# The second norm's root moved behind the first twelve up tiles of a hybrid decoder layer

## The reference

```python
    x = x + gate1 * (merged @ w_out)
    h2 = rms_norm(x, g_norm2) * (1.0 + scale2) + shift2
    x = x + gate2 * (jnp.square(jax.nn.relu(h2 @ w_up)) @ w_down)
```

## Time and profile before

| | us |
|---|---|
| runs shown (3) | 993.21, 993.28, 996.12; median 993.28 |
| profiled execution, its own time | 994.64 |
| profiled execution, span from first to last instruction | 992.9 |
| TensorE busy | 944.4 |
| VectorE busy | 497.6 |
| ScalarE busy | 391.0 |
| mean granted TensorE clock | 0.981 |

### The profile page before, as it was taken

One profiled execution on the slowest core, in us unless ns is written; L12 is line 12 of the kernel. 1 busy time (PEld: TensorE's weight loads), 2 busy tenths in 40 slices (PEclk: granted clock), 3 DMA queues, 4 the chain that ended last, 5 costly groups with the idle time before them and its releaser, 6 DMA issues.

```text
span 992.9 us, 19815 instructions
## 1 busy us (share of the span) xinstructions
PE 944.4 (95%) x7546; PEld 862.0 (87%) x7546; DVE 497.6 (50%) x1154; ACT 391.0 (39%) x813; POOL 139.5 (14%) x139
## 2 busy tenths in 40 slices
PE   8889989889899989899999999999999999999998
PEld 7588667767688768798799998999999999999997
DVE  3454767845625678861147556544332244443232
ACT  3254545555556646433333323433311233441121
POOL 4100232141334564310000000000000000000000
PEclk9889999999999989999999999999999999999999
DMA  9536764253422564587423331333223323322312
GB/s 322 186 107 194 185 226 129 96 160 124 132 65 73 167 207 131 158 256 252 143 65 95 98 86 43 85 87 103 86 86 102 87 85 90 100 85 88 103 43 86
DMA packets 176233, 124.54 MB, mean 125 GB/s; under 512 B 14739, under 2 KB 152019, under 8 KB 176164
## 3 DMA queue, kind: packets, MB, share of 16 engines
q1 hardware_dynamic: 176034, 123.50, 40.9%
q10 hardware_dynamic: 130, 0.10, 0.0%
HBM read 116.99 MB, written 6.59 MB: 124 GB/s over the span
## 4 chain that ended last, share of the span: by engine, by line
PE 66%; issue 20%; DVE 9%; ACT 3%; POOL 1%; POOLq 0%; ACTq 0%; DVEq 0%
PE bank L949 18%; PE bank L950 17%; PE bank L951 17%; PE bank L1030 2%; PE bank L1053 2%; PE bank L856 2%; PE bank L1039 2%; PE bank L1009 1%; PE bank L1071 1%; DVE sel L1878 1%; PE bank L878 1%; PE bank L1015 1%; PE bank L1094 1%; PE bank L1084 1%; DVE lg L1905 1%
## 5 line engine op out<-in xcount | busy, mean ns | idle before, releaser
L949 PE MATMUL bank<-h_hi,w_hi 128*128 128x260 f32 x1360 | 397.5, 292 | 8.0 <-DVE h_lo L1762 6.0
L950 PE MATMUL bank<-h_lo,w_hi 128*128 128x260 f32 x1360 | 388.5, 286 | 0.0
L951 PE MATMUL bank<-h_hi,w_lo 128*128 128x260 f32 x1360 | 388.1, 285 | 0.0
L949 PEld LDWEIGHTS bank<-h_hi,w_hi 128*128 128x128 f32 x1360 | 260.1, 191 | 31.6 <-issue 24.0
L951 PEld LDWEIGHTS bank<-h_hi,w_lo 128*128 128x128 f32 x1360 | 260.5, 192 | 0.0
L950 PEld LDWEIGHTS bank<-h_lo,w_hi 128*128 128x128 f32 x1360 | 260.2, 191 | 0.0
L949 PE MATMUL bank<-u_hi,w_hi 128*128 128x260 f32 x512 | 145.2, 284 | 0.0
L950 PE MATMUL bank<-u_lo,w_hi 128*128 128x260 f32 x512 | 144.8, 283 | 0.0
L951 PE MATMUL bank<-u_hi,w_lo 128*128 128x260 f32 x512 | 144.8, 283 | 0.0
L2213 DVE TENSOR_TENSOR w_lo<-raw,w_hi 128x1024 fp32r<-128x1024 f32 x62 | 76.0, 1226 | 135.2 <-ACT w_hi L1638 135.2
L1638 ACT ACTIVATE w_hi<-raw 128x1024 fp32r<-128x1024 f32 x62 | 65.4, 1055 | 140.3 <-PE bank L951 140.3
(11 more groups left out here) (316 smaller groups left out, 1180.9 us busy)
## 6 DMA issues: line engine op xcount, KB each, us to landing
raw<-in_w_in SPq DMA_DIRECT2D x44, 512.0 KB, 4.0
part<-in_w_ada SPq DMA_DIRECT2D x32, 512.0 KB, 5.4
raw<-in_w_up SPq DMA_DIRECT2D x32, 512.0 KB, 4.1
raw<-in_w_down SPq DMA_DIRECT2D x32, 512.0 KB, 4.1
ada<-in_w_ada SPq DMA_DIRECT2D x4, 2048.0 KB, 13.7
kv<-in_cache_k_b SPq DMA_DIRECT2D x16, 256.0 KB, 4.3
qbc<-q_d SPq DMA_DIRECT2D x16, 256.0 KB, 4.5
kv<-in_cache_k_a SPq DMA_DIRECT2D x16, 256.0 KB, 4.2
```

Source lines behind the costliest of these rows:

```text
L949: mm(out, hi[:, k, :], x_h, start=first and k == ks[0], stop=False)
L950: mm(out, hi[:, k, :], x_l, start=False, stop=False)
L951: end = mm(out, lo[:, k, :], x_h, start=False, stop=last and k == ks[-1])
```

## The change

The norm is rewritten around the product. With r the root of a token, W the up weights and s the scale times `g_norm2`, h2 W = r · ((x·s) W) + shift W. So twelve up tiles (`N_UNNORMED`) multiply x·s, without the root, and the root comes in afterwards, on the sums.

- **Inputs.** `scale_half` multiplies each chunk of `x_t` by `amul` inside the round of the `w_out` tile that made it. ScalarE rounds it to `h2_hi` there; the remainder `h2_lo` of the first half is taken in the same round, that of the second half in the next tile's (`rest_half`). Ten more columns (`N_C`) in front hold the shift, so the first half of such a tile has 270 columns, the second 260.
- **Order on TensorE.** Up tile 0 runs alone and chunk by chunk, with `norm_sums` between its chunks 4 and 5. `spread_roots` stands between the halves of up tile 1. `warm` is gone behind the sums.
- **Results.** VectorE takes the sums out of the bank with a multiply by `rs_row`, adds a correction for the 8 sample tokens, and ScalarE applies the ReLU with the shift as its bias.
- **The other up tiles.** `h3_hi` and `h3_lo`, which hold the normed inputs, are made chunk by chunk by both engines beside up tiles 2 to 10. Tiles 12 to 15 and the second quarter read them.
- **Weights.** `rest_w(T_MLP + 1)` stands ahead of `norm_root`, `rest_w(T_MLP + 2)` behind it. In the rounds of the `w_out` tiles ScalarE's `round_w` comes between the two halves.
- **Memory.** `u_hi` moves to the place of `h_hi` and `h_lo`.

```diff
@@ pe
-            norm_sums()
-            warm(10, 7)
-            spread_roots()
-            warm(8, 7)
+            def up_half(i, half, ks):
+                n0, n = (0, N_C + HALF) if half == 0 else (N_C + HALF, HALF)
+                out = bank[half + 4 * ((i + 1) % 2)][:, 0:n]
...
-            first_tiles(T_MLP, 1)
-            up_tile(0, 2, 0)
-            up_tile(0, 3, 0)
+            for i in (T_MLP, T_MLP + 1):
+                pe.wait_ge(hi_ready, i + 1)
+                pe.wait_ge(lo_ready, i + 1)
+                pe.wait_ge(dve_evac, 2 * (2 * NCH + i - T_MLP - 1))
+                if i == T_MLP:
+                    for k in range(NCH):
+                        pe.wait_ge(h2_lo_ready, 2 * k + 3)
+                        for half in range(2):
+                            up_half(i, half, [k])
+                        if k == 4:
+                            norm_sums()
+                else:
+                    up_half(i, 0, range(NCH))
+                    spread_roots()
+                    up_half(i, 1, range(NCH))
+            for n in range(2, N_UNNORMED):
+                pe.wait_ge(hi_ready, T_MLP + n + 1)
+                pe.wait_ge(lo_ready, T_MLP + n + 1)
+                for half in range(2):
+                    pe.wait_ge(u_evac, 2 * (n - 2) + half + 1)
+                    up_half(T_MLP + n, half, range(NCH))
+            pe.wait_ge(h3_lo_ready, NCH + 1)
             for q in range(2):
-                with pe.Fori(0 if q else 1, 4) as it:
+                with pe.Fori(0 if q else N_UNNORMED // 4, 4) as it:
@@ act
+                for half in range(2):
+                    if half and m < NCH - 1:
+                        round_w(i + 2)
+                    act.wait_ge(hf_ready, 2 * m + half + 1)
+                    A(h2_hi[:, m, ...], hf[:, m % 2, ...], ACT.Copy)\
+                        .then_inc(h2_hi_ready, 1)
+                square(m)
             round_w(T_MLP + 1)
-            round_h()
+            round_w(T_MLP + 2)
+            act.wait_ge(rs_spread2, 1)
+            A(rs_row[:, SEQ:T], bank[6][:, 0:NS], ACT.Copy)
+            A(rs_row[:, 0:SEQ], bank[3][:, :], ACT.Copy).then_inc(rs_kept, 1)
...
+            for n in range(N_UNNORMED):
+                if n:
+                    round_w(T_MLP + n + 2)
+                for half in range(2):
+                    if half == 0:
+                        act.wait_ge(u_evac, 2 * n + 1)
+                    else:
+                        act.wait_ge(z_ready, n + 1)
+                    uf = u_f[:, 2 * (n % 2) + half, :]
+                    A(uf, uf, ACT.Relu, bias=ws[:, n % 2, 0:1]).then_inc(act_evac, 1)
+                up_round(0, n % 4, n // 4)
...
@@ dve
                 for half in range(2):
                     dve.wait_ge(proj_done, 2 * (T_WO + g) + half + 1)
                     add_gated(bank[half + 4 * (g % 2)], half, slice(m, m + 1), slice(16 + m, 17 + m), m)
+                    scale_half(m, half)
+                    if half:
+                        rest_half(m, 0)
+                    elif m:
+                        rest_half(m - 1, 1)
...
+            rest_half(NCH - 1, 1)
+            rest_w(T_MLP + 1)
             norm_root()
-            norm_apply()
+            rest_w(T_MLP + 2)
+            dve.wait_ge(rs_kept, 1)
...
+            for n in range(N_UNNORMED):
+                first_up_tile(n)
+                if n:
+                    rest_w(T_MLP + n + 2)
+                up_squares(0, n % 4, n // 4)
+                j = n - 2
+                if j == 0:
+                    norm_samples()
+                if 0 <= j < NCH:
+                    norm_chunk(j)
+                up_rest(0, n % 4, n // 4)
+                if 0 <= j - 1 < NCH:
+                    rest_chunk(j - 1)
```

More of the change, by code:

```diff
@@ L1638, in round_loop, with up_round @@
                 A(w_hi[:, i % SPL], raw[:, i % RAW], ACT.Copy).then_inc(hi_ready, 1)
+            def up_round(q, b, it):
+                n = 32 * q + 2 * b
+                for half in range(2):
+                    act.wait_ge(u_sq, it * 8 + (n + half + 1))
+                    A(u_hi[:, bass.ds(it * 4 + b, 1), half * HALF:(half + 1) * HALF], u_f[:, 2 * (b % 2) + half:2 * (b % 2) + half + 1, :],
+                      ACT.Copy).then_inc(u_hi_ready, 1)
             def up_tile(q, b, it):
@@ L1653, in _ @@
             for q in range(2):
-                if q == 0:
+                with act.Fori(0 if q else N_UNNORMED // 4, 4) as it:
                     for b in range(4):
[L1656 to L1664, removed]
+                        up_tile(q, b, it)
@@ L1795, in scale_rows @@
                                        vec_t[:, 56:64].unsqueeze(2).to_broadcast([P, NCH, 9]), ALU.mult))
[L1797 to L1816, removed]
-                        dve.tensor_tensor(h_lo[:, :, SEQ:T], nsm[:, 0], h_hi[:, :, SEQ:T].bitcast(F32), ALU.subtract).then_inc(h_lo_ready, 1)
-                    else:
-                        dve.wait_ge(nf_ready, N_H + j + 1)
-                        rest_shifted(j - 1)
-                rest_shifted(NCH - 1)
@@ L2213, in rest_loop, with first_up_tile @@
                 dve.tensor_tensor(w_lo[:, i % SPL], raw[:, i % RAW], w_hi[:, i % SPL].bitcast(F32), ALU.subtract).then_inc(lo_ready, 1)
+            def first_up_tile(n):
+                i = T_MLP + n
+                at = 4 * ((i + 1) % 2)
+                for half in range(2):
+                    dve.wait_ge(proj_done, 2 * i + half + 1)
+                    if half == 0:
+                        dve.tensor_copy(ws[:, n % 2, :], bank[at][:, 0:N_C])
+                        acc = bank[at][:, N_C:N_C + HALF]
+                    else:
+                        acc = bank[at + 1][:, 0:HALF]
+                    dve.tensor_tensor(u_f[:, 2 * (n % 2) + half, :], acc, rs_row[:, half * HALF:(half + 1) * HALF], ALU.mult)\
+                        .then_inc(u_evac, 1)
+                dve.wait_ge(u_evac, 2 * n + 2)
+                us = u_f[:, 2 * (n % 2) + 1, HALF - NS:HALF]
+                dve.tensor_tensor(us, us, ws[:, n % 2, 1:9], ALU.add).then_inc(z_ready, 1)
@@ new lines, in up_squares, with up_rest @@
+            def up_squares(q, b, it):
+                for half in range(2):
+                    uf = u_f[:, 2 * (b % 2) + half, :]
+                    dve.wait_ge(act_evac, it * 8 + (2 * T_WO + 32 * q + 2 * b + half + 1))
+                    dve.tensor_tensor(uf, uf, uf, ALU.mult).then_inc(u_sq, 1)
+            def up_rest(q, b, it):
+                for half in range(2):
+                    slot = 2 * (b % 2) + half
+                    cols = slice(half * HALF, (half + 1) * HALF)
+                    dve.wait_ge(u_hi_ready, it * 8 + (32 * q + 2 * b + half + 1))
+                    dve.tensor_tensor(u_lo[:, bass.ds(it * 4 + b, 1), cols], u_f[:, slot:slot + 1, :],
+                                      u_hi[:, bass.ds(it * 4 + b, 1), cols].bitcast(F32), ALU.subtract).then_inc(u_lo_ready, 1)
@@ L2217, in _ @@
                     for b in range(4):
[L2218 to L2229 removed]
+                        up_squares(q, b, it)
```

190 lines of the change are left out of this document (120 added, 70 removed).

## The result

| | before | after |
|---|---|---|
| median of runs, us | 993.86 (992.70 to 997.54, 9 runs) | 986.61 (982.91 to 990.76, 9 runs) |
| ratio | | 0.9928, 95% interval 0.9912 to 0.9944 |
| profiled execution: time, span | 994.64, 992.9 | 986.4, 984.6 |

The kernel is 7.2 us faster by the medians and 8.3 by the two profiled spans. 982.5 was forecast, with a range of 980.5 to 985.8: the direction is right, the median lies 0.8 us above the range and 4.1 above the forecast. The fastest of the nine executions, 982.91, comes within half a microsecond of the forecast, but one execution is not what was forecast.

A forecast was written before the change was run, and what follows sets the result against it. TensorE bounds the kernel, busy 944.4 of 992.9 us; only its stops, filler and slow clock could be saved. A 29.38 us stretch becomes 17.3, saving 12.1, less 1.3 for wider matmuls: 993.28 − 10.8 = 982.5 us, range 980.5 to 985.8.

The forecast's parts named there:

- Both waits: TensorE's two large waits from 545 us on: 2.0 us ahead of an up tile's matmul, 1.7 us ahead of the roots' matmuls.
- the covers of 1.2 to 4.9 us: Time by which added steps come early enough: last chunk 4.9 us, root 1.8, evacuation of tiles 0 and 1 1.2, the tightest.
- Filler, sums, roots: TensorE between `w_out` and up tiles: identity matmuls as filler, to vanish; sums at 2.2 us and roots at 1.4 us stay.
- the second hole: TensorE's 2.18 us stop ahead of up tile 2, waiting for its split weights; with 1.6 us of clock, 3.8 us.
- the same 114 matmuls should run back to back: 114 × 0.120: The 96 matmuls of up tiles 0 and 1 and 18 of the third take 13.7 us without stops.
- the clock falls without a stop: Rival: TensorE's clock falls behind the one-column matmuls and roots without idleness; price 1.6 us, giving 984.1; chance 0.07.
- The wide matmuls: 288 matmuls in twelve up tiles with 270 columns in place of 260: 4.6 ns each, 1.3 us in all.
- the bounds given (0 to 2.9): Limits in us for the 270-column matmuls' cost: 0 if columns don't set the pace, 2.9 at 1 ns a column.
- The hole moves: Rival: a cover of 1.2 or 1.8 us is gone, TensorE stops 1 us plus 1.6 of clock: 985.1; chance 0.12.
- half of what it says: Rival: tile 2's weights still late behind `norm_root`, so 3.8 us are not saved: 986.3; chance 0.04.
- VectorE becomes the bound: Rival: VectorE needs 7.7 us a tile in up tiles 1 to 10, losing 14.9 us: 997.4; chance 0.04.

The follow-up runs named there:

- paired: Changed kernel with the old order of up tiles 0 and 1 put back, so both end at once: 992.37 us, ratio 0.9971 to the kernel before.
- aligned: Changed kernel with twelve columns in place of ten in front of the inputs (two unused), rows of 2128 bytes: 984.75 us, ratio 0.9910 to the kernel before.
- again: The changed kernel as it is, run a second time: 988.67 us, ratio 0.9942 to the kernel before.
- again_2: The changed kernel once more, as base of the last group of four: 986.22 us, ratio 0.9920 to the kernel before.
- narrow: Changed kernel whose first half of the twelve up tiles multiplies 260 columns, without the ten of the shift: 984.34 us, ratio 0.9903 to the kernel before.
- aligned_2: Changed kernel with twelve columns in place of ten, sums in one piece, run in the last group: 987.36 us, ratio 0.9935 to the kernel before.
- sums_spread: Changed kernel with the ten products of the sums placed one by one between half chunks of up tile 0: 985.91 us, ratio 0.9919 to the kernel before.

## Why the prediction was wrong

*The mechanism held.* Both waits went; no new wait came; the covers of 1.2 to 4.9 us were enough; VectorE kept up (34.5 us busy in tiles 3 to 9, 4.9 each as forecast). Filler, sums, roots and the second hole had their predicted prices. **paired** gives the last: 4.0 us by the profiles and 3.9 by the means, against 3.8. And where the clock stayed full, tile 2 starts when the prediction says: 15.4 us after the first up matmul in **aligned** (597.61 to 612.96), against 15.3.

*The step that failed is "the same 114 matmuls should run back to back: 114 × 0.120".* In the profile after, 15 of them ran at 1.2 GHz, and 1.5 us were lost. The prediction had this as its second rival, "the clock falls without a stop", with nearly the right price (1.6) and a chance of 0.07. Its argument against was that before, the clock stayed at full through the sums and fell only after idleness. That was one execution of one placing. Sums in one piece were followed by a low clock in three of six profiles (after, again, again_2; not narrow, aligned, aligned_2), and in both with sums doubled or tiles paired; sums spread or left out, in none of five. So it comes with the sums in one piece, but not in each profile; what decides is not shown.

*The wide matmuls were mis-sized:* 1.8 in place of 1.3, against the same base of 5.77 us a tile. The ten columns cost less than thought (3.5 ns a matmul, 1.0 us in all). The rest is a cost that the prediction did not have: about 0.06 us a tile for the rows of the new buffer, which start at other multiples, and a remainder that no run explains. It lies within the bounds given (0 to 2.9).

*What the two profiles add up to.* From the place of the sums to the end, the kernel before takes 394.7 us and the changed one 385.6: 9.1 saved where 10.8 was forecast. Of the 1.7 missing, 1.5 is the clock and 0.5 the wide matmuls. Tiles 12 to 15 and the sixteen up tiles of the second quarter gave back about 0.5, at 5.75 us and not 5.77, which was not forecast; the remaining 0.2 was lost behind the last tiles. The profiled spans differ by 8.3 and not by 9.1 because this execution of the changed kernel reached the place 0.85 us later (599.01 against 598.16), ahead of the change.

*The base moved.* 982.5 was taken from 993.28, the median of three executions; nine give 993.86. That is 0.6 of the 4.1 us between forecast and median. The remaining gap between the profiled pair (8.3) and the medians (7.2) is of the size of the scatter ahead of the change, and no run here resolves it further.

*The range was too narrow at its upper end.* It was built from the bounds of the sum. The three executions of before already spanned 2.9 us, and a median of such executions does not sit at one execution's sum; half of that spread on top of 985.8 would have reached 987. The fallen clock by itself was inside the range.

*Rivals.* "The hole moves", "half of what it says" and "VectorE becomes the bound" did not occur: VectorE's splits keep 5.92 us from tile to tile with idle time ahead of each.

## What to carry to other kernels

A normalisation's root can be moved from the inputs of a product to its sums. Here that left 3.5 us (sums and roots) of an 11.6 us serial stretch on TensorE's path, for the price of some columns and busier side engines. When such a hole is filled, read the granted clock of what fills it: thin matmuls in one piece are busy time that may still be followed by a slow stretch. And where variants differ by less than the executions scatter, give the range that scatter too. Decide between them by the time from the first changed instruction to the end: it repeated within 0.1 us here, where the medians of one kernel lay up to 2.6 apart.

## What was not expected of the hardware

- The clock fell to half with no idle time ahead of it, behind 2.1 us of one-column matmuls that TensorE's busy row counts in full (clock 0.71 from 603.9 to 609.7 in the profile after; five of the eight profiles with these matmuls in one piece).
- The same instructions ahead of the change (475 to 552 us) ran at full clock in one execution (sums_spread, 1.00) and for 6.8 us at half clock in another (after, 0.96).
- 260-column matmuls from rows 2120 bytes apart took 5.84 us a tile, from rows 2080 apart 5.75 (5.77 in the kernel before); with 272 columns and rows of 2128 bytes 5.88, less than 270 columns in rows of 2120 (5.92).
